# Encoder layer on eight cores: a smaller bias table expanded on the scalar engine, and normalising multiplies spread between attention items

## The chip, the cores and the metric

One Trainium2 chip, eight cores. The batch of 16 sequences is split by data: each core computes two whole sequences, one after the other, with its own copy of all weights, and exchanges nothing with the others. The time is the device time of the slowest core in microseconds. TensorE does the matrix products, VectorE (DVE) and ScalarE (ACT) the element-wise work and the copies out of PSUM, GpSimd (POOL) some element-wise work and the DMAs that change the type, and SyncE (SP) issues the other DMAs.

## The reference

Input x is 16 x 2048 x 1024, float32. One layer:

```
proj = x @ w_in                        # q, k, v of 24 heads, a Fourier branch, two gates
for g, (window, d) in ((128,1), (512,4), (2048,16)):     # 8 heads of 64 each
    query i sees keys i + m*d, |m| <= 64
    logits = q.k / 8 + bias[bucket(distance), head]
    out_g, lse_g = softmax(logits) @ v, log-sum-exp
attn = sum over g of softmax(lse)_g * out_g
four = real part of a 2-D DFT of the Fourier branch
mix  = (sig(gate_a) * (attn @ w_attn_out) + sig(gate_f) * (four @ w_fourier_out)) @ w_out
h    = layer_norm(alpha * x + mix)
out  = layer_norm(alpha * h + relu(h @ w_up + b_up)^2 @ w_down + b_down)
```

The merge of the three windows by their log-sum-exp equals one softmax over all keys of the three windows: numerators and denominators of the three can be added up and divided once at the end.

## The kernel before

A planner class records every operation with the buffers it reads and writes, and derives the semaphore waits from that; each engine then runs its list in the order in which the operations were recorded. Almost all operations go through small helpers, so most lines of the profile are those of a helper: 327 a matmul, 325 a matmul into a part of a bank, 330 a transpose, 316 and 317 a copy out of PSUM on ACT, 319 and 320 the same on DVE, 294 a DMA. SBUF is one pool with a stack of regions; a new region waits for the last users of whatever lay there before.

For each of the two sequences:

- x comes in 16 tiles of 128 tokens (SP queue, three buffers, 512 KB each). TensorE transposes a tile and, one tile later, multiplies it by the v weights of the first window (`v_chunk`, eight matmuls of 512 columns into one bank, copied out by ACT and DVE in turn). Two v weight blocks and the bias table are issued on the POOL queue ahead of that; the third v block needs the first one's buffer (lines 398 to 401).
- The bias table holds, for each of 24 heads, a block of 128 keys by 512 columns, with -30000 outside the band. A block of a head consists of two equal copies of 256 columns, for the widest window of four equal copies of 128. It is float32 in HBM and becomes bfloat16 in the DMA. After the first window's V, ACT takes the exponential of the whole table in place (line 432), then V of the other two windows follows, 16 chunks each.
- Attention runs over 12 pairs of heads: for each of four rounds `pp`, the windows g = 0, 1, 2. Before the items of a pair, TensorE runs the first two of its score products and then the q and k projection of the following pair (`proj`, 64 matmuls, evicted into `qk` by ACT and DVE in turn). An item is a bank of scores: TensorE computes it two items ahead, ACT takes the exponential (line 538), DVE multiplies it by the table (line 542), TensorE multiplies V by it (65 rows: 64 outputs and the denominator), and finished stretches of 512 positions are merged by DVE into `acc` (lines 570, 574, 579) one item later. A pair has 16 items for g = 0 and 1, 8 for g = 2.
- After the third window of a round, the denominators go through DRAM (`norm_dma`): stored, loaded as a 128 x 32 block, inverted on DVE, stored, and broadcast to 64 partitions in `rbc`. Eight multiplies of 64 x 512 (`norm_mul`, line 471) write `attnT`. They are recorded in the next pair, behind its projection and ahead of its items; for the fourth round, at the end of the attention stage.
- The q and k weights of each pair (`wqk`) come on the POOL queue with two buffers. In sequence 0 each of the first loads is followed by a cast of MLP weights from DRAM to DRAM (8 MB results for two of the three), in the same queue.
- Then the Fourier branch, the gated merge, the output projection, the layer norms and the MLP; they are not touched.

Of the kernel before, what the change touches and what calls it, by code (L numbers as in the profile page):

```python
# [7 lines left out]
BF16 = mybir.dt.bfloat16  # L8
AF = mybir.ActivationFunctionType
ALU = mybir.AluOpType  # L10
# [8 lines left out]
NEG = -30000.0  # L19
# [212 lines left out]
def build(debug=None, nseq=NSEQ):  # L232
    nc = bass.Bass("TRN2", target_bir_lowering=False)
    kb = KB(nc)
    mem = Mem(nc)

    def din(name, shape, dt=F32):
        return nc.dram_tensor(name, list(shape), dt, kind="ExternalInput").ap()
# [8 lines left out]
    wout_d = din("wout", [128, 8, D])  # L247
    wup_d = din("wup", [8, 128, 8, 512])
    wdn_d = din("wdn", [8, 128, 32, 128])
    tab_d = din("tab", [128, 24, 512])  # L250
    dft_d = din("dft", [4, 2, 128, 8, 512], BF16)
    c1024_d = din("c1024", [1, S], BF16)
    ccsc_d = din("ccsc", [128, 256], BF16)
# [30 lines left out]
    identf, identf_r, _ = palloc("identf", F32, [128])  # L284
    identb, identb_r, _ = palloc("identb", BF16, [128])
    onesf, onesf_r, _ = palloc("onesf", F32, [64])
    ccsc, ccsc_r, _ = palloc("ccsc", BF16, [256])
    pvec, pvec_r, _ = palloc("pvec", F32, [72])
    g2b, g2b_r, _ = palloc("g2b", F32, [D])
    b2b, b2b_r, _ = palloc("b2b", F32, [D])  # L290
    mhalf, mhalf_r, _ = palloc("mhalf", F32, [8])

    def dma(eng, out, in_, reads=(), writes=(), is_out=False):
        return kb.op(eng, lambda e: e.dma_start(out=out, in_=in_), reads, writes, dma=True, is_out=is_out)
# [78 lines left out]
    try:  # L373
        for s in range(nseq):
            mem.mark()
            mem.mark()
            xT, xT_r, _ = palloc("xT", BF16, [8, S], nres=16)
            attnT, attnT_r, _ = palloc("attnT", BF16, [4, S], nres=4)
            wf, wf_r, _ = palloc("wf", BF16, [8, 512], nres=1)

            xs, xs_r, _ = palloc("xs", F32, [3, D], nres=3, high=True)
            xs_ring = Ring(16, 3, lambda k, b: dma("sp", xs[:, b, :], x_d[s, k * 128:(k + 1) * 128, :],
                                                   writes=[xs_r[b]]))
# [9 lines left out]
            tab, tab_r, _ = palloc("tab", BF16, [24, 512])  # L393
            V, V_r, _ = palloc("V", BF16, [3, 16, 8, 65], nres=3)
# [3 lines left out]
            wv, wv_r, _ = palloc("wv", BF16, [2, 8, 512], nres=2)  # L398
            wv_ring = Ring(3, 2, lambda k, b: dma("pool", wv[:, b], wv_d[k], writes=[wv_r[b]]))
            wv_ring.need(0)  # L400
            dma("pool", tab, tab_d, writes=tab_r)

            def v_chunk(g, d, nkc, c):
                seg, kc = c // nkc, c % nkc
# [11 lines left out]
            for tt in range(16):  # L416
                xs_ring.need(tt)
                b = tt % 3
                for half in range(2):
                    bk, br = next_bank()  # L420
# [8 lines left out]
            v_chunk(0, 1, 16, 15)  # L429
            if debug is not None and debug[0] == "xT" and s == 0:  # L430
                finish_debug(xT, xT_r)
            kb.op("act", lambda e: e.activation(out=tab, in_=tab, func=AF.Exp), tab_r, tab_r)
            for g, (win, d) in enumerate(GROUPS):
                if g == 0:
                    continue
# [29 lines left out]
                dma("sp", rbc.rearrange("p e t -> p (e t)"), rden_s.to_broadcast([64, 2 * S]), reads=rden_sr, writes=rbc_r)  # L465

            def norm_mul(pp_):
                for e2 in range(2):
                    for tq in range(4):
                        cs = slice(tq * 512, (tq + 1) * 512)  # L470
                        kb.op("dve", (lambda cs, e2: lambda e: e.tensor_tensor(  # L471
                            out=attnT[64 * e2:64 * e2 + 64, pp_, cs], in0=acc[0:64, e2, cs], in1=rbc[:, e2, cs],
                            op=ALU.mult))(cs, e2), [acc_r[e2]] + rbc_r, [attnT_r[pp_]])

            pt_cnt = [0]
            pending_norm = None
# [2 lines left out]
            def proj(k):  # L479
                d = GROUPS[pairs[k][1]][1]  # L480
                wb = k % 2
                wqk_ring.need(k)
                for which in range(2):
                    for tq in range(4):
                        bk, br = next_bank()
                        for dc in range(8):
                            mm(bk[:, :], wqk[:, wb, which, dc, :], xT[:, dc, tq * 512:(tq + 1) * 512],
                               dc == 0, dc == 7, xT_r + [wqk_r[wb]], [br])
                        dst = qk[:, wb, which, :].rearrange("p (r l) -> p r l", r=d)[:, :, tq * 512 // d:(tq + 1) * 512 // d]
                        src = bk[:, :].rearrange("p (m r) -> p r m", r=d)  # L490
                        evac_copy(dst, src, [br], [qk_r[wb * 2 + which]], scale=(0.125 if which == 0 else None))
                        bfree(br)

            proj(0)
            for pair_i, (pp, g) in enumerate(pairs):
                if True:
# [96 lines left out]
                        it[0][1](it[1])  # L593
                    if pair_i + 1 < len(pairs):
                        proj(pair_i + 1)
                    if pending_norm is not None:
                        norm_mul(pending_norm)
                        pending_norm = None
                    pend = []
                    for ii, it in enumerate(items):  # L600
                        if ii + LA < len(items):
                            nx = items[ii + LA]
                            nx[0][1](nx[1])
                        pb = pt_cnt[0] % 3
                        pt_cnt[0] += 1
                        it[0][2](it[1], pb)
                        for mfn in pend:
                            mfn()
                        pend = []
                        it[0][3](it[1], pb, pend)  # L610
                    for mfn in pend:
                        mfn()
                if g == 2:
                    norm_dma()
                    pending_norm = pp
            norm_mul(pending_norm)
            mem.release()
            if debug is not None and debug[0] == "attnT" and s == 0:
                finish_debug(attnT, attnT_r)
# [330 lines left out]
def host_inputs(x, rel_bias, w_in, w_fourier_out, w_attn_out, w_out, ln1_g, ln1_b, w_up, b_up, w_down, b_down,  # L950
                ln2_g, ln2_b):
    f32 = np.float32
    w_in = np.asarray(w_in, f32)[0]
    Q, K_, V_, F_, GA, GF = 0, 1536, 3072, 4608, 5120, 6144

    def tile_w(w):
        return np.ascontiguousarray(w.reshape(8, 128, -1).transpose(1, 0, 2))

    wqk = np.stack([np.stack([tile_w(w_in[:, Q + 128 * p:Q + 128 * (p + 1)]),
                              tile_w(w_in[:, K_ + 128 * p:K_ + 128 * (p + 1)])]) for p in range(12)])  # L960
    wv = np.stack([tile_w(w_in[:, V_ + 512 * g:V_ + 512 * (g + 1)]) for g in range(3)])
    wf = tile_w(w_in[:, F_:F_ + 512])
    wg = np.stack([tile_w(w_in[:, GA + 128 * i:GA + 128 * (i + 1)]) for i in range(16)])
    wao = np.ascontiguousarray(np.asarray(w_attn_out, f32)[0].reshape(4, 128, D).transpose(1, 0, 2))
    wfo = np.ascontiguousarray(np.asarray(w_fourier_out, f32)[0].reshape(4, 128, D).transpose(1, 0, 2))
    wout = tile_w(np.asarray(w_out, f32)[0])
    wu = np.asarray(w_up, f32)[0]
    wup = np.stack([tile_w(wu[:, 512 * i:512 * (i + 1)]) for i in range(8)])
    wd = np.asarray(w_down, f32)[0]
    wdn = np.stack([np.ascontiguousarray(wd[:, 128 * dc:128 * (dc + 1)].reshape(32, 128, 128).transpose(1, 0, 2))  # L970
                    for dc in range(8)])
    rb = np.asarray(rel_bias, f32)
    i = np.arange(128)[:, None]
    j = np.arange(256)[None, :]
    rel = i - j + 64
    valid = np.abs(rel) <= 64
    tab = np.empty((128, 24, 512), f32)
    for g, (win, d) in enumerate(GROUPS):
        bk = t5_buckets(rel * d)
        for hh in range(8):  # L980
            h = 8 * g + hh
            t_ = np.where(valid, rb[bk, h], f32(NEG))
            if d == 16:
                tab[:, h, :] = np.tile(t_[:, 64:192], (1, 4))
            else:
                tab[:, h, :] = np.tile(t_, (1, 2))
    n = np.arange(S, dtype=np.int64)
    ang = 2.0 * np.pi * ((n[:, None] * n[None, :]) % S).astype(np.float64) / S
    cs = np.stack([np.cos(ang), np.sin(ang)]) / np.sqrt(S)
    c1024 = np.ascontiguousarray(cs[0, S // 2:S // 2 + 1, :]).astype(ml_dtypes.bfloat16)  # L990
    dft = cs[:, :S // 2].reshape(2, 8, 128, 4, 512).transpose(3, 0, 2, 1, 4)
    dft = np.ascontiguousarray(dft).astype(ml_dtypes.bfloat16)
    m = np.arange(128, dtype=np.int64)
    a2 = 2.0 * np.pi * ((m[:, None] * m[None, :]) % 128).astype(np.float64) / 128
    ccsc = (np.concatenate([np.cos(a2), -np.sin(a2)], axis=1) / np.sqrt(128.0)).astype(ml_dtypes.bfloat16)
    identf = np.eye(128, dtype=f32)
    identb = np.eye(128).astype(ml_dtypes.bfloat16)

    def pp(v):
        return np.asarray(v, f32).reshape(-1, 128).T  # L1000

    g1, b1 = np.asarray(ln1_g, f32)[0], np.asarray(ln1_b, f32)[0]
    pvec_parts = [pp(g1), pp(b1), None, None, pp(np.asarray(b_down, f32)[0]), pp(np.asarray(b_up, f32)[0])]
    shared = dict(wqk=wqk, wv=wv, wf=wf, wg=wg, wao=wao, wfo=wfo, wout=wout, wup=wup, wdn=wdn, tab=tab, dft=dft,
                  ccsc=ccsc, c1024=c1024, identf=identf, identb=identb,
                  g2b=np.ascontiguousarray(np.broadcast_to(np.asarray(ln2_g, f32)[0], (128, D))),
                  b2b=np.ascontiguousarray(np.broadcast_to(np.asarray(ln2_b, f32)[0], (128, D))))
    return shared, pvec_parts
# [26 lines left out]
```

How the kernel before makes its waits and increments, by code:

```python
        def run(e, eng):  # L119
            waited = {}
            for o in self.ops[e]:
                for d in o.deps:
                    if d.dma:
                        key, sem, val = ("d", d.sem), dsem[d.sem], d.val
                    else:
                        key, sem, val = ("e", d.eng), esem[d.eng], d.val
                    if waited.get(key, 0) >= val:
                        continue
                    waited[key] = val
                    eng.wait_ge(sem, val)
                ins = o.fn(eng)
                if o.dma:
                    ins.then_inc(dsem[o.sem], 16)
                elif o.signal:
                    ins.then_inc(esem[e], 1)
            if e == "sp":
                for sem, val in final_waits:
                    eng.wait_ge(sem, val)
```

## Time and profile before

| what | value |
|---|---|
| median of 10 runs | 2910.73 us (2907.38 to 3274.39) |
| profiled execution | 2907.47 us |
| its span on the slowest core (core 4) | 2905.9 us; the cores lie between 2883.3 and 2905.9 |
| TensorE matmul busy | 2465.3 us, 85% |
| DVE, ACT, POOL busy | 1138.6 (39%), 736.9 (25%), 153.8 (5%) |
| chain that ended last | PE 77%, DVE 8%, issue 5%, DMA 5%, ACT 2% |

The profile is one execution, seen from its slowest core. Busy time counts an engine's instructions; the chain follows the work that ended last back through its releasers. Matmuls are pipelined, so a busy TensorE is not one at its peak. An idle time before an instruction is given with what ended it, as far as semaphores show. The granted clock of TensorE is 1.00 at 2.4 GHz and 0.50 at 1.2 GHz; a stretch that shows something between has parts at both.

### The profile page before, as it was taken

How to read it: one execution, taken by the hardware profiler on the slowest of the kernel's cores; microseconds unless marked ns; L12 is line 12 of the kernel's file. 1: busy time of each engine (PE TensorE's matmuls, PEld its weight loads, DVE VectorE, ACT ScalarE, POOL GpSimd, SP SyncE). 2: the span in 40 equal slices, each digit the busy share in tenths (PEclk: the TensorE clock that was granted, in tenths of full speed). 3: DMA queues.
4: the chain of work that ended last, by engine and by line, in shares of the span. 5: the costliest groups of instructions: out<-in, count | busy, mean ns of one | idle time of the engine just before them, and what ended most of it. 6: DMA issues, size and time to landing. Idle time of an engine off the chain costs nothing.

```text
span 2905.9 us, 44223 instructions; the slowest of 8 cores (2883.3 to 2905.9 us)
## 1 busy us (share of the span) xinstructions
PE 2465.3 (85%) x11571; PEld 1168.3 (40%) x11784; DVE 1138.6 (39%) x2021; ACT 736.9 (25%) x1272; POOL 153.8 (5%) x189
## 2 busy tenths in 40 slices
PE   2884588887998999999946988888799989999995
PEld 1441233343443444444423533333344434444442
DVE  0222245542335345454321245545314454445442
ACT  0321132231222323232103132223212243223230
POOL 0000000000000001011010000000000000101011
PEclk9986777778999999999979977777899989999998
DMA  7699402124312244344355111100431133435342
GB/s 162 106 112 111 69 11 37 23 30 118 101 23 80 109 138 176 144 160 145 146 126 122 36 17 36 30 16 15 103 138 23 42 118 129 165 144 182 124 146 101
DMA packets 52442, 277.14 MB, mean 95 GB/s; under 512 B 7578, under 2 KB 7834, under 8 KB 30620
## 3 DMA queue, kind: packets, MB, share of 16 engines
q1 hardware_dynamic: 38676, 215.58, 21.5%
q0 software_dynamic: 13520, 58.72, 14.5%
q8 instruction: 101, 1.65, 0.2%
q14 instruction: 145, 1.19, 0.1%
HBM read 315.96 MB, written 35.91 MB: 121 GB/s over the span
## 4 chain that ended last, share of the span: by engine, by line
PE 77%; DVE 8%; issue 5%; DMA 5%; another core or an unknown queue 2%; ACT 2%; POOL 1%; DVEq 0%; SPq 0%; ACTq 0%; POOLq 0%
PE bank L327 67%; PE bank L325 7%; DMA pool<-x 2%; PE bank L330 2%; DVE pool L542 2%; DVE pool L471 1%; DVE pool L319 1%; ACT pool L316 1%; DVE pool L579 1%; ACT pool L538 1%; DMA pool<-den_s 1%; DMA pool<-rden_s 1%; DVE pool L764 1%; DMA pool<-wv 0%
## 5 line engine op out<-in xcount | busy, mean ns | idle before, releaser
L327 PE MATMUL bank<-pool 128*128 128x512 bf16 x9035 | 2059.6, 387 | 176.2 <-DMA pool<-wqk 69.7
L327 PEld LDWEIGHTS bank<-pool 128*128 128x128 bf16 x9248 | 930.3, 101 | 1276.3 <-issue 268.7
L325 PE MATMUL bank<-pool 64*128 64x256 bf16 (+7 forms) x1768 | 318.8, 322 | 137.1 <-DVE pool L542 112.8
L319 DVE CAST pool<-bank 128x512 bf16<-128x512 f32 x160 | 110.0, 693 | 495.0 <-PE bank L327 318.5
L325 PEld LDWEIGHTS bank<-pool 64*128 64x128 bf16 (+2 forms) x1768 | 144.4, 126 | 313.6 <-issue 306.1
L884 DVE TENSOR_SCALAR pool<-bank,pool 128x512 f32<-128x512 f32 x256 | 186.9, 748 | 172.9 <-PE bank L327 158.5
L316 ACT ACTIVATE pool<-bank 128x512 bf16<-128x512 f32 (+1 forms) x194 | 114.9, 597 | 530.0 <-PE bank L327 396.4
L888 ACT ACTIVATE pool<-pool 128x512 bf16<-128x512 f32 x256 | 160.2, 628 | 315.4 <-DVE pool L884 156.7
L538 ACT ACTIVATE pool<-bank 128x448 bf16<-128x448 f32 (+1 forms) x320 | 179.5, 570 | 200.6 <-PE bank L325 171.2
L330 PE MATMUL bank<-pool 128*128 128x128 f32 x768 | 107.2, 287 | 98.3 <-DMA pool<-x 79.3
L899 DVE SCALAR_TENSOR_TENSOR pool<-bank,pool 128x512 f32<-128x512 f32 x64 | 48.1, 751 | 328.1 <-PE bank L327 255.7
L330 PEld LDWEIGHTS bank<-pool 128*128 128x128 f32 x768 | 95.5, 149 | 118.4 <-issue 103.6
L715 ACT ACTIVATE pool<-bank 128x512 bf16<-128x512 f32 x128 | 76.2, 597 | 247.3 <-PE bank L327 244.4
L542 DVE TENSOR_TENSOR pool<-pool 128x448 bf16<-128x448 bf16 (+1 forms) x320 | 121.7, 403 | 33.8 <-ACT pool L538 32.8
L320 DVE TENSOR_SCALAR pool<-bank 128x512 bf16<-128x512 f32 x48 | 33.2, 691 | 238.0 <-PE bank L327 238.0
L723 DVE TENSOR_TENSOR pool<-bank,pool 128x512 f32<-128x512 f32 x64 | 44.3, 692 | 181.9 <-PE bank L327 181.9
L816 ACT ACTIVATE pool<-bank,pool 128x128 bf16<-128x128 f32 (+1 forms) x256 | 92.3, 469 | 51.3 <-PE bank L330 51.3
L317 ACT ACTIVATE pool<-bank 128x512 bf16<-128x512 f32 x48 | 28.7, 597 | 289.8 <-PE bank L327 289.8
L799 ACT ACTIVATE pool<-pool 128x1024 f32<-128x1024 f32 x32 | 39.7, 1240 | 223.1 <-DVE pool L775 223.1
L860 ACT ACTIVATE pool<-bank,pool 128x512 f32<-128x512 f32 x32 | 24.9, 778 | 255.4 <-DVE pool L856 198.6
L772 POOL TENSOR_TENSOR pool<-pool 128x1 f32<-128x1 f32 x64 | 35.1, 548 | 1028.6 <-DVE pool L769 1028.6
L822 DVE TENSOR_SCALAR pool<-bank,pool 128x128 bf16<-128x128 f32 (+1 forms) x256 | 84.4, 401 | 5.4 <-PE bank L330 2.7
(43 smaller groups left out, 683.4 us busy)
## 6 DMA issues: line engine op xcount, KB each, us to landing
pool<-wup_s SPq DMA_DIRECT2D x64, 1024.0 KB, 5.3
pool<-wdn_s SPq DMA_DIRECT2D x64, 1024.0 KB, 4.8
pool<-x SPq DMA_DIRECT2D x64, 512.0 KB, 4.0
pool<-dft SPq DMA_DIRECT2D x16, 1024.0 KB, 4.9
out<-pool SPq DMA_DIRECT2D x32, 512.0 KB, 2.9
pool<-wqk POOLq DMA_DIRECT2D x24, 512.0 KB, 6.5
wup_s<-wup POOLq DMA_DIRECT2D x1, 8192.0 KB, 117.6
wdn_s<-wdn POOLq DMA_DIRECT2D x1, 8192.0 KB, 132.0
```

Of the source, the lines that this page charges most:

```text
L316: return kb.op("act", lambda e: e.activation(out=out, in_=in_, func=AF.Copy), reads, writes)
L319: return kb.op("dve", lambda e: e.tensor_copy(out=out, in_=in_), reads, writes)
L325: return kb.op("pe", lambda e: e.matmul(out, lhsT, rhs, start=start, stop=stop, skip_group_check=True), reads, writes)
L327: return kb.op("pe", lambda e: e.matmul(out, lhsT, rhs, start=start, stop=stop), reads, writes)
L330: return kb.op("pe", lambda e: e.transpose(out, in_, identf), list(reads) + identf_r, writes)
L538: kb.op("act", lambda e: e.activation(out=PT[:, pb, c0:c1], in_=bk[:, c0:c1], func=AF.Exp), [br], [PT_r[pb]])
L542: kb.op("dve", lambda e: e.tensor_tensor(out=PT[:, pb, c0:c1], in0=PT[:, pb, c0:c1], in1=tcols, op=ALU.mult), [PT_r[pb]] + tab_r, [PT_r[pb]])
L715: kb.op("act", (lambda bk, gbuf, af: lambda e: e.activation(out=gts[:, gbuf, af, :], in_=bk[:, :], func=AF.Sigmoid))(bk, gbuf, af), [br], ...
L816: kb.op("act", (lambda bk, j, dc, dst, so, bo: lambda e: e.activation(out=dst, in_=bk[:, j * 128:(j + 1) * 128], func=AF.Identity, scale=p ...
L822: kb.op("dve", (lambda bk, j, dc, dst, so, bo: lambda e: e.tensor_scalar(out=dst, in0=bk[:, j * 128:(j + 1) * 128], scalar1=pvec[:, so + d ...
L884: kb.op("dve", (lambda bk, rb, fc: lambda e: e.tensor_scalar(out=rr[:, rb, :], in0=bk[:, :], scalar1=pvec[:, BUP + fc:BUP + fc + 1], scala ...
L888: kb.op("act", (lambda rb, fc: lambda e: e.activation(out=hidT[:, fc, :], in_=rr[:, rb, :], func=AF.Square))(rb, fc), [rr_r[rb]], [hidT_r[ ...
```

## The change

The table in HBM has one copy of 256 columns per head (24 x 256 in place of 24 x 512 per partition). It is loaded, still with the type changed in the DMA, into a new buffer `tabraw`, allocated behind `wv` and released with it; `qk` comes to lie on the same bytes later. The DMA is recorded after the first window's V, and on POOL's list it still stands between the second and the third v block. The single exponential becomes six: two write the two copies of the 16 heads of the first two windows (16 x 256 columns each), four write the four copies for the widest window from the middle 128 columns (8 x 128 columns each). All six write one resource of the planner.

`norm_mul` returns the eight multiplies as a list. In the pair that follows, two are taken from the list after the exponential and table multiply of each item and ahead of the pending merges, so that they are spread over the first four items. At the end of the attention stage they are run at once.

```
--- before.py
+++ after.py
@@ -247,7 +247,7 @@
     wout_d = din("wout", [128, 8, D])
     wup_d = din("wup", [8, 128, 8, 512])
     wdn_d = din("wdn", [8, 128, 32, 128])
-    tab_d = din("tab", [128, 24, 512])
+    tab_d = din("tab", [128, 24, 256])
     dft_d = din("dft", [4, 2, 128, 8, 512], BF16)
     c1024_d = din("c1024", [1, S], BF16)
     ccsc_d = din("ccsc", [128, 256], BF16)
@@ -398,7 +398,7 @@
             wv, wv_r, _ = palloc("wv", BF16, [2, 8, 512], nres=2)
             wv_ring = Ring(3, 2, lambda k, b: dma("pool", wv[:, b], wv_d[k], writes=[wv_r[b]]))
             wv_ring.need(0)
-            dma("pool", tab, tab_d, writes=tab_r)
+            tabraw, tabraw_r, _ = palloc("tabraw", BF16, [24, 256])
 
             def v_chunk(g, d, nkc, c):
                 seg, kc = c // nkc, c % nkc
@@ -429,7 +429,15 @@
             v_chunk(0, 1, 16, 15)
             if debug is not None and debug[0] == "xT" and s == 0:
                 finish_debug(xT, xT_r)
-            kb.op("act", lambda e: e.activation(out=tab, in_=tab, func=AF.Exp), tab_r, tab_r)
+            dma("pool", tabraw, tab_d, writes=tabraw_r)
+            for i in range(2):
+                kb.op("act", (lambda i: lambda e: e.activation(out=tab[:, 0:16, 256 * i:256 * i + 256],
+                                                                in_=tabraw[:, 0:16, :], func=AF.Exp))(i),
+                      tabraw_r, tab_r)
+            for i in range(4):
+                kb.op("act", (lambda i: lambda e: e.activation(out=tab[:, 16:24, 128 * i:128 * i + 128],
+                                                                in_=tabraw[:, 16:24, 64:192], func=AF.Exp))(i),
+                      tabraw_r, tab_r)
             for g, (win, d) in enumerate(GROUPS):
                 if g == 0:
                     continue
@@ -465,12 +473,14 @@
                 dma("sp", rbc.rearrange("p e t -> p (e t)"), rden_s.to_broadcast([64, 2 * S]), reads=rden_sr, writes=rbc_r)
 
             def norm_mul(pp_):
+                fns = []
                 for e2 in range(2):
                     for tq in range(4):
                         cs = slice(tq * 512, (tq + 1) * 512)
-                        kb.op("dve", (lambda cs, e2: lambda e: e.tensor_tensor(
+                        fns.append((lambda cs, e2: lambda: kb.op("dve", lambda e: e.tensor_tensor(
                             out=attnT[64 * e2:64 * e2 + 64, pp_, cs], in0=acc[0:64, e2, cs], in1=rbc[:, e2, cs],
-                            op=ALU.mult))(cs, e2), [acc_r[e2]] + rbc_r, [attnT_r[pp_]])
+                            op=ALU.mult), [acc_r[e2]] + rbc_r, [attnT_r[pp_]]))(cs, e2))
+                return fns
 
             pt_cnt = [0]
             pending_norm = None
@@ -593,8 +603,9 @@
                         it[0][1](it[1])
                     if pair_i + 1 < len(pairs):
                         proj(pair_i + 1)
+                    norm_fns = []
                     if pending_norm is not None:
-                        norm_mul(pending_norm)
+                        norm_fns = norm_mul(pending_norm)
                         pending_norm = None
                     pend = []
                     for ii, it in enumerate(items):
@@ -604,6 +615,9 @@
                         pb = pt_cnt[0] % 3
                         pt_cnt[0] += 1
                         it[0][2](it[1], pb)
+                        for _ in range(2):
+                            if norm_fns:
+                                norm_fns.pop(0)()
                         for mfn in pend:
                             mfn()
                         pend = []
@@ -613,7 +627,8 @@
                 if g == 2:
                     norm_dma()
                     pending_norm = pp
-            norm_mul(pending_norm)
+            for fn_ in norm_mul(pending_norm):
+                fn_()
             mem.release()
             if debug is not None and debug[0] == "attnT" and s == 0:
                 finish_debug(attnT, attnT_r)
@@ -974,16 +989,12 @@
     j = np.arange(256)[None, :]
     rel = i - j + 64
     valid = np.abs(rel) <= 64
-    tab = np.empty((128, 24, 512), f32)
+    tab = np.empty((128, 24, 256), f32)
     for g, (win, d) in enumerate(GROUPS):
         bk = t5_buckets(rel * d)
         for hh in range(8):
             h = 8 * g + hh
-            t_ = np.where(valid, rb[bk, h], f32(NEG))
-            if d == 16:
-                tab[:, h, :] = np.tile(t_[:, 64:192], (1, 4))
-            else:
-                tab[:, h, :] = np.tile(t_, (1, 2))
+            tab[:, h, :] = np.where(valid, rb[bk, h], f32(NEG))
     n = np.arange(S, dtype=np.int64)
     ang = 2.0 * np.pi * ((n[:, None] * n[None, :]) % S).astype(np.float64) / S
     cs = np.stack([np.cos(ang), np.sin(ang)]) / np.sqrt(S)
```

## Rows read from the trace of the kernel before

**Rows 1.** Page, costliest groups: names, shapes, count; busy us, mean ns; idle, releaser.

```profile
L327 PE MATMUL bank<-pool 128*128 128x512 bf16 x9035 | 2059.6, 387 | 176.2 <-DMA pool<-wqk 69.7
```

**Rows 2.** Waits of TensorE: waiter, releaser: us in total, times, longest us.

```profile
PE bank L325 <- DVE pool L542: 112.8, 118, 7.2
PE bank L330 <- DMA pool<-x: 79.3, 3, 44.3
```

**Rows 3.** Chain of waits, 0 to 420 us: start us, length us, what.

```profile
4.38 39.70 DMA pool<-x
...
119.65 10.74 PE bank L327 x49
...
270.22 45.06 another core or an unknown queue
```

**Rows 4.** Timeline of POOL, to 420 us: start, us, instruction [idle, releaser].

```profile
2.84 0.55 POOL L294 DMA_DIRECT2D pool<-tab  x1
110.86 0.53 POOL L294 DMA_DIRECT2D pool<-wv  x1 [107.48 <-PE bank L327]
```

**Rows 5.** DMA issues, to 60 us: count, KB each, us to landing.

```profile
pool<-tab POOLq DMA_DIRECT2D x1, 3072.0 KB, 38.3
```

**Rows 6.** Transfers of the tile wv, 0 to 60 us, issue to landing.

```profile
DMA to landing us min/median/max: 11.4/14.6/17.8
```

**Rows 7.** DMA queues, 20 to 28 us: packets, MB, time share.

```profile
q0 software_dynamic: 48, 1.18, 84.6%
q1 hardware_dynamic: 49, 0.20, 10.9%
```

**Rows 8.** DMA issues by line, 1490 to 1560 us.

```profile
pool<-tab POOLq DMA_DIRECT2D x1, 3072.0 KB, 23.1
```

**Rows 9.** Chain of waits, 1440 to 1640 us.

```profile
1517.38 22.35 DMA pool<-x
```

**Rows 10.** Timeline of TensorE, 1495 to 1545 us.

```profile
1539.87 1.94 PE L330 MATMUL bank<-pool 128*128 128x128 f32 x8 [11.51 <-DMA pool<-x]
```

**Rows 11.** Timeline of ACT, 104 to 135 us.

```profile
108.75 0.60 ACT L316 ACTIVATE pool<-bank 128x512 bf16<-128x512 f32 x1 [2.98 <-PE bank L327]
109.24 10.44 ACT L432 ACTIVATE pool<-pool 128x12288 bf16<-128x12288 bf16 x1
119.58 0.60 ACT L316 ACTIVATE pool<-bank 128x512 bf16<-128x512 f32 x1
```

**Rows 12.** Timeline of ACT, 1583 to 1615 us.

```profile
1586.52 0.60 ACT L316 ACTIVATE pool<-bank 128x512 bf16<-128x512 f32 x1 [2.98 <-PE bank L327]
...
1598.78 0.58 ACT L316 ACTIVATE pool<-bank 128x512 bf16<-128x512 f32 x1
```

**Rows 13.** Timeline of all engines, 336 to 384 us.

```profile
358.69 6.19 DVE L471 TENSOR_TENSOR pool<-pool 64x512 bf16<-64x512 f32 x8
364.92 1.06 DVE L542 TENSOR_TENSOR pool<-pool 128x448 bf16<-128x448 bf16 x3
...
365.46 15.15 PE L325 MATMUL bank<-pool 128*65 128x192 bf16 x68 [7.23 <-DVE pool L542]
...
370.23 0.69 DVE L570 COPY pool<-bank 65x512 f32<-65x512 f32 x1 [0.19 <-PE bank L325]
```

**Rows 14.** Timeline of all engines, 192 to 212.5 us.

```profile
196.30 2.81 PE L325 MATMUL bank<-pool 128*65 128x192 bf16 x19 [0.99 <-DVE pool L542]
...
199.74 0.69 DVE L570 COPY pool<-bank 65x512 f32<-65x512 f32 x1 [0.16 <-PE bank L325]
```

**Rows 15.** Transfers that read rden_s, 348 to 350 us, issue to landing.

```profile
DMA to landing us min/median/max: 9.0/9.0/9.0
```

**Rows 16.** Stretch: us, busy by engine, granted clock, DMA share, GB/s.

```profile
365.40:370.00 4.60, 4.54 (x21) 1.88 (x22) 2.42 (x6) 1.79 (x3) 0.00 (x0) 0.50 0.00 0
```

**Rows 17.** The same view, in the pair without a pending normalisation.

```profile
200.00:202.00 2.00, 2.00 (x11) 0.78 (x10) 1.30 (x4) 0.91 (x2) 0.00 (x0) 0.50 1.81 197
```

**Rows 18.** The same view, in a dense stretch of the MLP.

```profile
1200.00:1400.00 200.00, 196.98 (x939) 95.36 (x956) 98.94 (x185) 57.54 (x101) 26.87 (x28) 0.99 0.44 158
```

More of the change, by code:

```diff
@@ L249, in build @@
     wdn_d = din("wdn", [8, 128, 32, 128])
-    tab_d = din("tab", [128, 24, 512])
+    tab_d = din("tab", [128, 24, 256])
     dft_d = din("dft", [4, 2, 128, 8, 512], BF16)
@@ L400, in build @@
             wv_ring.need(0)
-            dma("pool", tab, tab_d, writes=tab_r)
+            tabraw, tabraw_r, _ = palloc("tabraw", BF16, [24, 256])
             def v_chunk(g, d, nkc, c):
@@ L431, in build @@
                 finish_debug(xT, xT_r)
-            kb.op("act", lambda e: e.activation(out=tab, in_=tab, func=AF.Exp), tab_r, tab_r)
+            dma("pool", tabraw, tab_d, writes=tabraw_r)
+            for i in range(2):
+                kb.op("act", (lambda i: lambda e: e.activation(out=tab[:, 0:16, 256 * i:256 * i + 256],
+                                                                in_=tabraw[:, 0:16, :], func=AF.Exp))(i),
+                      tabraw_r, tab_r)
+            for i in range(4):
+                kb.op("act", (lambda i: lambda e: e.activation(out=tab[:, 16:24, 128 * i:128 * i + 128],
+                                                                in_=tabraw[:, 16:24, 64:192], func=AF.Exp))(i),
+                      tabraw_r, tab_r)
             for g, (win, d) in enumerate(GROUPS):
@@ L467, in norm_mul @@
             def norm_mul(pp_):
+                fns = []
                 for e2 in range(2):
@@ L470, in norm_mul @@
                         cs = slice(tq * 512, (tq + 1) * 512)
-                        kb.op("dve", (lambda cs, e2: lambda e: e.tensor_tensor(
+                        fns.append((lambda cs, e2: lambda: kb.op("dve", lambda e: e.tensor_tensor(
                             out=attnT[64 * e2:64 * e2 + 64, pp_, cs], in0=acc[0:64, e2, cs], in1=rbc[:, e2, cs],
-                            op=ALU.mult))(cs, e2), [acc_r[e2]] + rbc_r, [attnT_r[pp_]])
+                            op=ALU.mult), [acc_r[e2]] + rbc_r, [attnT_r[pp_]]))(cs, e2))
+                return fns
             pt_cnt = [0]
@@ L595, in build @@
                         proj(pair_i + 1)
+                    norm_fns = []
                     if pending_norm is not None:
-                        norm_mul(pending_norm)
+                        norm_fns = norm_mul(pending_norm)
                         pending_norm = None
@@ L606, in build @@
                         it[0][2](it[1], pb)
+                        for _ in range(2):
+                            if norm_fns:
+                                norm_fns.pop(0)()
                         for mfn in pend:
@@ L615, in build @@
                     pending_norm = pp
-            norm_mul(pending_norm)
+            for fn_ in norm_mul(pending_norm):
+                fn_()
             mem.release()
@@ L976, in host_inputs @@
     valid = np.abs(rel) <= 64
-    tab = np.empty((128, 24, 512), f32)
+    tab = np.empty((128, 24, 256), f32)
     for g, (win, d) in enumerate(GROUPS):
@@ L981, in host_inputs @@
             h = 8 * g + hh
[L982 to L986, printed above, removed]
+            tab[:, h, :] = np.where(valid, rb[bk, h], f32(NEG))
     n = np.arange(S, dtype=np.int64)
```

## The prediction

> **What bounds the kernel now.** I read the page's list of costly groups first, to see what fills the time, then TensorE's waits, to see what it lacks, then the chain of waits and the timelines around the two places that the diff touches. The 9035 matmuls of line 327 hold 2059.6 of 2905.9 us [rows 1]; so whatever opens a gap in TensorE's stream is paid in full, and other engines matter only through such gaps. Of the gaps [rows 2], two belong to this change: 79.3 us in three waits for x tiles, and 112.8 us in 118 waits for line 542, the multiply by the bias table, with a longest of 7.2 us. A third kind, the wait for wqk behind the long cast jobs, the diff leaves alone, but it stands between the first gap and the end and must be followed.
>
> **The table's transfer, sequence 0.** TensorE starts when the first x tile lands, at 4.38 + 39.70 = 44.1 us [rows 3]. What holds a tile of 512 KB for 40 us? The table was issued at 2.84 [rows 4] and landed 38.3 us later, at 41.1 [rows 5]; the second wv load, issued just before it at about 2.3, took 17.8 us and landed near 20.1 [rows 6]. Between them the two queues moved 48 and 49 packets, but 1.18 MB against 0.20 [rows 7]: the engines take one packet from each in turn, a table packet (a row of 24 KB) is six times an x packet (4 KB), and so x and the two 512 KB constants ahead of it crawl until the table is through. With half the bytes the table still has 128 packets, one per partition, but of 12 KB. So as many packets of the other queue pass, and only the table's own time halves: 41.1 - 20.1 = 21.0 us, less the 10.9% in which the other queue moved [rows 7], 18.7, half of it 9.3. I take 9, since some of a landing does not shrink with the bytes.
>
> Does that reach the end? V of the first window follows at TensorE's pace, its end frees the wv buffer, and only then POOL issues the third wv load (110.86) with the casts behind it [rows 4]. That queue runs through to the fourth wqk load, for which TensorE stands 45.06 us from 270.22, until 315.3 [rows 3]. The queue begins 9 us earlier and ends 9 us earlier. The table's place on POOL's list is the same (after two wv loads, ahead of the third), so nothing is moved past anything there.
>
> The Trainium skill, DMA: Bandwidth & Descriptors, Anatomy of one DMA, fits 2.0 us plus bytes over 436 GB/s: by that the 1.57 MB saved in SBUF are worth 3.6 us a time, 7 for both sequences instead of 18. The trace moves 3.15 MB in some 18.7 us, 168 GB/s in SBUF bytes, and decides against it; the float source is twice as many bytes.
>
> **Sequence 1.** The same table takes 23.1 us [rows 8]; an x tile issued at 1517.38 lands 22.35 us later [rows 9], and TensorE stands idle for 11.51 us of that, until 1539.87 [rows 10]. Half of 23.1 less 10.9% is 10.3; I take 9 again. It stays below the 11.51 us of gap, so all of it counts, and after it no queue is late. Bounds for both together: 15 to 21 us, taken 18.
>
> **The expansion.** One activation of 128x12288 took 10.44 us from 109.24; the next eviction on ACT came at 119.58 [rows 11]. Six pieces hold as many elements. Each writes the whole table's resource, so each waits for the one before; five more starts at about 0.3 us (0.17 of fixed time, what the 0.60 us of an eviction of 512 columns holds beyond the slope of the long one, and a round through the own semaphore) make 1.5 us. What hides it: TensorE fills eight banks in rotation at 8 x 10.74/49 = 1.75 us each [rows 3], and the bank that ACT empties at 120.2 is needed again at 124.4 (the first chunk of the second window starts at 108.6, just before the eviction of the last chunk of the first at 108.75; that bank comes round again nine chunks on). That is 4.2 us of cover, in sequence 1 about 2.8 (1598.78 + 0.58 = 1599.4, against 1586.4 + 9 x 1.75 = 1602.2) [rows 12]. Cost nothing; a full microsecond more per piece would cost some 5 us in all. The raw table's bytes become part of qk's, so the first evictions into qk wait for the expansion, which ended 40 us before. The lower end: nothing is gained here.
>
> **The multiplies.** At the first pair of each later round, DVE runs eight multiplies of 0.68 us in one block of 6.19 us from 358.69, then three table multiplies in 1.06; TensorE idles 7.23 us until 365.46 [rows 13]. The same rows stand six times, three per sequence; the blocks at the ends of the sequences are drained at once as before. After the change DVE runs a table multiply, then two normalising ones, four times over. Start to start, from [rows 13]: table to normalising 0.33 ((1.06 - 0.41)/2), normalising to normalising 0.79, normalising to table 0.72: 1.84 a round. From 358.69, four rounds end at 366.05; the first merge into acc (0.69, line 570) follows, as it must, behind the last normalising multiply, and the fifth table multiply starts at 366.7 and ends at 367.1. The fifth item's P.V then ends at 367.7. Before, the merge that waits for that product started at 370.23, so it ended about 370.1. From there on TensorE is without gaps in both cases. Gain 2.4 to 2.5 us, not 7.2: DVE still owes 6.2 us before item five, and the items can lend it little idle time. Six times: 15 us.
>
> Bounds. If a table multiply does not overlap with its neighbours, a round is 2.1 us and the gain 1.5. The upper end is the pair without a pending normalisation: its same merge came at 199.74, 4.4 us after TensorE fell idle behind the projection (196.30 - 0.99) [rows 14], against 12.0 here (370.23 after 365.46 - 7.23): 7.6 us. The added wait: the first normalising multiply now sits behind one table multiply on DVE, and the later table multiplies behind it; it needs the broadcast reciprocals, issued at 348.66 and landed 9.0 us later, at 357.7 [rows 15], 1.3 us before it is due at 359.0. So it holds nothing up. TensorE's clock: after the stall it is granted 0.50, the 1.2 GHz level [rows 16]; with TensorE only trickling I expect the same fall.
>
> **Sum.** Against the profiled run (2907.5 us, span 2905.9): 18 + 15 = 33, giving 2874.5. That run lies 3.3 us below the median of 2910.7; on the median's scale 2878.
>
> **Rivals.**
> Starts only: DVE's total decides and the interleaved items end where they did; 2910.7 - 18 = 2893. For it: DVE has the same work to do. Against: today TensorE must catch up from 365.46, at the low clock, on work that could have been done meanwhile.
> Clock held: if TensorE, never idle for long, keeps the 2.4 GHz level, the pair costs what the one without normalisation does; 18 + 6 x 7.6 = 64, giving 2847. Against: after a gap of only 1 us the pair of [rows 14] falls to 0.50 too [rows 17].
> Transfer less halved: a large fixed part in the table's landing, starts worth 7 rather than 18; 22 in all, giving 2889.
> Slower: fuller cores are granted less clock. Place: the long dense stretches, now at 0.99 [rows 18]. Price: line 327's 2059.6 us [rows 1] at 0.97 instead of 1.00 cost 64 us, less 33 is 31 more, 2942; it decides from about 0.985. Against: dense stretches of 200 us ran at 0.99, and only 1% of idle time is taken out. The Trainium skill, TensorE: Matmul & The Clock Gate, Part 1, says that a die with three cores on dense matmuls is held at 13/16; that speaks for this one, and no dense stretch here shows it.
> Not as said: the x tile is held by the constants rather than the table and the multiplies stay tied to one another; no change, 2911. The packet counts speak against it.
>
> **How the numbers follow.** Forecast 0.65, starts only 0.14, clock held 0.07, transfer less halved 0.05, slower 0.05, no change 0.04. Faster by over 0.2% (5.8 us, about what a measurement of this kernel can tell from no change): 0.65 + 0.14 + 0.07 + 0.05 = 0.91; same 0.04; slower 0.05. The forecast's own range is 15 to 21 plus six times 1.5 to 3.5, so 24 to 42: 2869 to 2887. The range for 8 in 10 reaches up over the two weaker gains to 2897 and down half way to the held clock, 2860.
>
> **What would show it.** The first x tile lands at about 35 us, the table at 32; the wait for the fourth wqk load ends near 306; in sequence 1 the gap before tile five is near 2.5 us; TensorE never waits for ACT at the second window's V. At the six pairs, four rounds of one table and two normalising multiplies 1.84 us apart, TensorE's gaps about 1 us each, the next projection 2.5 us sooner. I am wrong if x still lands after 40 us, if the fifth P.V ends no sooner relative to the projection's end, or if the dense stretches show a clock under 0.98.

## The result, and the profile after

The changed kernel took 2872.94 us (median of 9 runs) where the kernel before took 2910.66 (32 runs): ratio 0.9861, 95% interval 0.985 to 0.9871, some 40 us. The forecast was 33 less, 2878. In some executions the cores of a die show a lower granted clock and take longer (the first profile of the changed kernel is one: 0.81 on core 3 from 2600 to 2800 us), and the ratios here leave those out, which is why the two medians differ by only 37.7. The rows below are from a second profile of the same kernel, a run of its own (2862.72 us, ratio 0.9862, 0.9843 to 0.9881), core 1, its slowest.

The page, and under it TensorE's waits (total us, times, longest us), answer to [rows 1, 2]:

```profile
span 2860.2 us, 44215 instructions; the slowest of 8 cores (2844.4 to 2860.2 us)
...
L327 PE MATMUL bank<-pool 128*128 128x512 bf16 x9248 | 2078.7, 387 | 154.0 <-DMA pool<-wqk 65.7
```

```profile
PE bank L325 <- DVE pool L552: 102.8, 145, 1.8
PE bank L327 <- DMA pool<-wqk: 65.7, 2, 43.3
PE bank L330 <- DMA pool<-x: 58.8, 4, 34.0
```

Line 552 is the old 542, the multiply by the table. Its longest wait fell from 7.2 to 1.8 us, while the sum only fell from 112.8 to 102.8: more and shorter waits. x cost 20.5 us less. A matmul of line 327 still lasts 387 ns, and the dense stretches of the MLP are granted 0.99 and 1.00 (the column behind the engines' busy times), as before [rows 18]:

```profile
1200.00:1400.00 200.00, 195.85 (x943) 93.72 (x942) 99.31 (x185) 59.60 (x104) 26.88 (x28) 0.99 0.41 148
2600.00:2800.00 200.00, 195.84 (x947) 93.50 (x946) 91.86 (x170) 56.39 (x99) 23.26 (x24) 1.00 0.42 151
```

Sequence 0: the chain, and the issues of the first 60 us (KB of one, median us to landing), which answer to [rows 3, 5, 6]:

```profile
4.59 29.16 DMA pool<-x
...
258.08 43.20 another core or an unknown queue
301.41 15.97 PE bank L327 x64
```

```profile
pool<-wv POOLq DMA_DIRECT2D x2, 1024.0 KB, 14.2
pool<-tab POOLq DMA_DIRECT2D x1, 1536.0 KB, 27.8
```

The first x tile lands at 33.75 instead of 44.1, the table 27.8 us after issue instead of 38.3, and the wait for the fourth wqk load ends at 301.4 instead of 315.3. The two queues from 20 to 28 us (packets, MB, share), as in [rows 7]:

```profile
q0 software_dynamic: 96, 1.16, 82.8%
q1 hardware_dynamic: 98, 0.39, 17.9%
```

Still one packet for one: in the same 8 us the table's queue moved 1.16 MB where it had moved 1.18, now in 96 packets of 12 KB, and the other queue got 98 turns instead of 49.

POOL's DMA issues (first the third wv load of sequence 0, then the loads of sequence 1) and, under them, TensorE in sequence 1 at the sixth tile, which the prediction calls tile five, counting from 0 (start, length, what, idle before and its releaser; [rows 10] before).

```profile
100.94 0.53 POOL L294 DMA_DIRECT2D pool<-wv  x1 [97.56 <-PE bank L327]
...
1471.86 1.17 POOL L294 DMA_DIRECT2D pool<-wv  x2 [3.56 <-PE bank L330]
1473.01 0.55 POOL L294 DMA_DIRECT2D pool<-tab  x1
```

```profile
1498.66 1.89 PE L327 MATMUL bank<-pool 128*128 128x512 bf16 x8 [1.20 <-ACT pool L316]
1501.58 1.06 PE L330 MATMUL bank<-pool 128*128 128x128 f32 x8 [1.03 <-DMA pool<-x]
```

The gap is 1.03 us instead of 11.51 (over the eight cores 0.83 to 2.42 instead of 9.99 to 13.11). From the first V matmul to the table's exponential it is 64.6 us (1484.58 to 1549.16), before 75.4 (1512.99 to 1588.43).

ACT at the expansion, against [rows 11]:

```profile
99.31 7.32 ACT L434 ACTIVATE pool<-pool 128x4096 bf16<-128x4096 bf16 x2
106.72 4.50 ACT L438 ACTIVATE pool<-pool 128x1024 bf16<-128x1024 bf16 x4
111.13 0.58 ACT L316 ACTIVATE pool<-bank 128x512 bf16<-128x512 f32 x1
```

Six pieces in 11.8 us, 1.4 over the single piece of 10.44. From 96 to 180 us TensorE has no wait for ACT, and none from 1545 to 1600 us in sequence 1.

The first of the six pairs, all engines in order of time, against [rows 13] (L480 is the normalising multiply, L580 the merge):

```profile
344.66 0.39 PE L325 MATMUL bank<-pool 64*128 64x256 bf16 x2
...
345.51 0.38 DVE L552 TENSOR_TENSOR pool<-pool 128x448 bf16<-128x448 bf16 x1
345.81 1.47 DVE L480 TENSOR_TENSOR pool<-pool 64x512 bf16<-64x512 f32 x2
...
347.20 0.41 DVE L552 TENSOR_TENSOR pool<-pool 128x512 bf16<-128x512 bf16 x1
347.53 1.46 DVE L480 TENSOR_TENSOR pool<-pool 64x512 bf16<-64x512 f32 x2
...
347.75 0.70 PE L325 MATMUL bank<-pool 128*65 128x256 bf16 x5 [1.05 <-DVE pool L552]
...
352.83 0.69 DVE L580 COPY pool<-bank 65x512 f32<-65x512 f32 x1
353.44 0.75 DVE L552 TENSOR_TENSOR pool<-pool 128x512 bf16<-128x512 bf16 x2
...
354.41 0.69 DVE L580 COPY pool<-bank 65x512 f32<-65x512 f32 x1 [0.22 <-PE bank L325]
```

One table multiply, two normalising ones, a round every 1.69 to 1.96 us, and TensorE waits about 1 us in each. TensorE's granted clock over the pair (the column behind the engines' busy times; the last two are DMA):

```profile
344.70:349.00 4.30, 1.72 (x12) 0.67 (x11) 3.89 (x8) 1.59 (x3) 0.70 (x1) 1.00 0.50 74
349.00:352.00 3.00, 1.46 (x9) 0.68 (x10) 2.80 (x5) 0.80 (x2) 0.00 (x0) 0.64 0.37 69
352.00:366.00 14.00, 12.34 (x57) 4.88 (x57) 9.91 (x22) 5.81 (x10) 0.00 (x0) 0.50 0.00 1
```

It falls to 0.50, the 1.2 GHz level, as it did before [rows 16]: the held clock did not come.

### The profile page after: what moved, and what is told of

Read it like the earlier page. It is cut to its first block, busy times and chain, and to the rows that moved or that the text cites. A ratio compares the mean times of both kernels' runs of the same rounds, so it can differ in the third digit from the quotient of the medians.

```text
span 2911.7 us, 44215 instructions; the slowest of 8 cores (2869.7 to 2911.7 us)
## 1 busy us (share of the span) xinstructions
PE 2521.8 (87%) x11784; PEld 1178.9 (40%) x11784; DVE 1137.8 (39%) x2021; ACT 741.0 (25%) x1282; POOL 153.8 (5%) x189
## 4 chain that ended last, share of the span: by engine, by line
PE 78%; DVE 7%; issue 5%; DMA 4%; another core or an unknown queue 2%; ACT 2%; POOL 1%; DVEq 0%; SPq 0%; ACTq 0%; POOLq 0%
PE bank L327 70%; PE bank L325 6%; PE bank L330 2%; DVE pool L552 2%; DMA pool<-x 2%; DVE pool L319 1%; DVE pool L480 1%; DVE pool L589 1%; ACT pool L316 1%; ACT pool L548 1%; DMA pool<-den_s 1%; DMA pool<-rden_s 1%; DMA den_s<-pool 0%; DVE pool L779 0%
## 5 line engine op out<-in xcount | busy, mean ns | idle before, releaser
L327 PE MATMUL bank<-pool 128*128 128x512 bf16 x9248 | 2126.4, 393 | 155.0 <-DMA pool<-wqk 67.6
L327 PEld LDWEIGHTS bank<-pool 128*128 128x128 bf16 x9248 | 940.4, 102 | 1307.1 <-issue 421.5
L325 PE MATMUL bank<-pool 64*128 64x256 bf16 (+7 forms) x1768 | 311.8, 317 | 126.3 <-DVE pool L552 102.9
```

The costliest lines, as they stand in the source:

```text
L325: return kb.op("pe", lambda e: e.matmul(out, lhsT, rhs, start=start, stop=stop, skip_group_check=True), reads, writes)
L327: return kb.op("pe", lambda e: e.matmul(out, lhsT, rhs, start=start, stop=stop), reads, writes)
```

## The experiments

Diffs are against the changed kernel. Gains are the ratio's distance from 1 times about 2908 us, the median of before beside these runs.

**The changed kernel once more** (full_again), beside its halves. No edit.

> The whole change once more, beside its two halves on the same chip. Sum theory (table and multiplies each keep their own gain): 38 to 42 us below before, as first measured. For the profile: the first x tile lands at 35 us; in sequence 1 TensorE waits less than 1 us for the x tile that cost it 11.5 us, because POOL issues the raw table right behind the two wv loads; the 15.9 us that POOL spent ahead of the old table's DMA are gone.

Ratio 0.9862 (0.9843 to 0.9881), 40 us: what the halves below must add up to.

**The table alone** (table_only): small table and expansion, all eight multiplies in one block.

```
-                        norm_fns = norm_mul(pending_norm)
+                        for fn_ in norm_mul(pending_norm):
+                            fn_()
```

> The small table with its expansion, the eight multiplies in one block as before. Sum theory: 9 us at the start of sequence 0 and 11 at the start of sequence 1, some 20 us below before (ratio 0.993). Rival, the multiplies bring nothing and the table all of it: 40 us below (0.986). Rival, the table's fixed part dominates: 7 us below (0.9975).

2886.1 us, ratio 0.9935 (0.992 to 0.9949): 18.9 us; the block is back (6.19 us on DVE, TensorE idle for 7.23). The table's term was 18.

**The multiplies alone** (multiplies_only): the old table and its single exponential, the multiplies spread.

```
-    tab_d = din("tab", [128, 24, 256])
+    tab_d = din("tab", [128, 24, 512])
-            tabraw, tabraw_r, _ = palloc("tabraw", BF16, [24, 256])
+            dma("pool", tab, tab_d, writes=tab_r)
...
+            kb.op("act", lambda e: e.activation(out=tab, in_=tab, func=AF.Exp), tab_r, tab_r)
```

> The spread multiplies with the old table. Sum theory: 2.4 us at each of six pairs, 15 us below before (0.995); if the measured 40 us is all to be shared by the two halves, up to 20 us. Rival, DVE's total decides and spreading moves nothing: within 2 us of before. Rival, the pair falls back to the cost of one without pending multiplies: 45 us below (0.985).

2883.31 us, ratio 0.993 (0.9914 to 0.9945): 20.4 us, where the term was 15. The halves sum to 39 of 40: they don't share a gain. "Starts only" (18 in all) falls, and "transfer less halved" (7 for the starts) falls with the run before.

**One multiply per item** (one_per_item): over eight items instead of four.

```
-                        for _ in range(2):
+                        for _ in range(1):
```

> The whole change, but one multiply after each of the first eight items in place of two after each of the first four. Theory (DVE's start-to-start times set the rounds): a round is 0.33 + 0.72 = 1.05 us, under the 1.1 us that TensorE needs for an item at its lower clock, so DVE no longer holds TensorE up; the pair ends some 2.5 us sooner than with two per item, 15 us in all, ratio to before 0.981. Rival, only DVE's total of 6.2 us counts: as the whole change, 0.986. Rival, the clock then holds longer as well: 0.976 or less.

2847.8 us, ratio 0.9799 (0.9783 to 0.9816): 58.5 us, 18 more than the changed kernel. DVE and TensorE (core 2) at the first pair:

```profile
345.63 0.38 DVE L552 TENSOR_TENSOR pool<-pool 128x448 bf16<-128x448 bf16 x1
345.93 0.68 DVE L480 TENSOR_TENSOR pool<-pool 64x512 bf16<-64x512 f32 x1
346.53 0.41 DVE L552 TENSOR_TENSOR pool<-pool 128x512 bf16<-128x512 bf16 x1
```

```profile
347.08 0.70 PE L325 MATMUL bank<-pool 128*65 128x256 bf16 x5 [0.26 <-DVE pool L552]
348.02 0.71 PE L325 MATMUL bank<-pool 128*65 128x64 bf16 x5 [0.24 <-DVE pool L552]
```

For the first four items a round is 0.9 us, an item's P.V 0.70, TensorE's gaps 0.25 instead of 1.05. From the fifth item on a merge joins the multiplies on DVE, and TensorE waits again, 1.01, 0.68 and 0.65 us; the clock falls as with two per item (0.65 from 349 to 352 us, then 0.50):

```profile
350.68 2.26 PE L325 MATMUL bank<-pool 128*65 128x64 bf16 x10 [1.01 <-DVE pool L552]
```

From the pair's first score products to the next pair's it is 34.9 us; with two per item 37.6 (344.66 to 382.24), with the block 40.6 (357.85 to 398.49). So what bounds the interleaved items is DVE's list between two table multiplies, as the prediction had it, and the later items have room for more of it, though not for all: "DVE no longer holds TensorE up" holds for the first four items only.

**The table issued late again** (late_issue). The trace after showed something that the prediction had not: before, POOL let 16 us pass in sequence 1 between the wv loads and the table. POOL, the kernel before, core 4:

```profile
1499.28 1.17 POOL L294 DMA_DIRECT2D pool<-wv  x2 [3.56 <-PE bank L330]
1516.37 0.53 POOL L294 DMA_DIRECT2D pool<-tab  x1 [15.91 <-PE bank L327]
```

After, the table follows wv at once. The old buffer overlaps buffers that the MLP of sequence 0 had used, and in the kernel's lists its load carries 257 semaphore waits; `tabraw` lies elsewhere, and its load carries 2. To see whether the waits make the 16 us, and whether the 16 us make the gain, the small table's load gets the old buffer's dependencies as well:

```
-            dma("pool", tabraw, tab_d, writes=tabraw_r)
+            dma("pool", tabraw, tab_d, writes=tabraw_r + tab_r)
```

> The whole change, but the raw table's DMA also declared a writer of the table's buffer, so that in sequence 1 POOL again passes 257 waits, all long satisfied, ahead of it. Theory (the 15.91 us that POOL stood ahead of the old table's DMA in sequence 1, on all cores alike, are those waits at some 62 ns each): POOL is idle about 15.9 us between the wv loads and the raw table, the table lands later, and TensorE waits 2 to 4 us for the x tile instead of 1. Rival (the 15.91 us were a full descriptor ring or a fetch held up by traffic): POOL issues the table right away, as in the whole change.

This run has no ratio; its trace is read, on core 4:

```profile
1484.49 0.53 POOL L294 DMA_DIRECT2D pool<-tab  x1 [16.03 <-PE bank L327]
```

```profile
1478.56 3.16 PE L327 MATMUL bank<-pool 128*128 128x512 bf16 x8 [10.91 <-DMA pool<-wv]
...
1499.54 1.06 PE L330 MATMUL bank<-pool 128*128 128x128 f32 x8 [1.93 <-DMA pool<-x]
```

The 16 us are back on all eight cores, 16.03 on each, whatever TensorE is doing there, so the waits make them. But they cost nothing: the sixth tile comes in time, the seventh 1.93 us late (1.03 and, on core 4, 2.42 us at the sixth in the changed kernel), and from the first V matmul (1478.56) to the exponential (1543.23) it is 64.7 us, as in the changed kernel (64.6, on core 4 64.8). I had taken the earlier issue for a part of the gain in sequence 1; that falls. With the half size the gap closes wherever the load is issued.

**x first** (x_first). In sequence 0 TensorE still stands 34 us for x. Four constants are moved behind the first x loads, and the table waits for the ninth transposed x tile:

```
-    dma("sp", g2b, g2b_d, writes=g2b_r)
-    dma("sp", b2b, b2b_d, writes=b2b_r)
...
+            if s == 0:
+                rest_consts()
...
-            dma("pool", tabraw, tab_d, writes=tabraw_r)
+            dma("pool", tabraw, tab_d, reads=[xT_r[8]], writes=tabraw_r)
```

> The whole change, with the first x tiles ahead of the constants that are needed late, and the raw table's load held back until the ninth x tile has been transposed. Theory (queues take turns packet by packet, so what counts is how many packets stand ahead of x and how large the other queue's are): the first x tile lands at 14 to 16 us instead of 34, the next two within 6 us; sequence 0 gains some 18 us, sequence 1 one; ratio 0.979 to 0.981. Rival, the software queue goes first altogether: x lands when the second wv load is through, 20 us, gain 14 us. Rival, the held-back table now comes late for its exponential or starves later x tiles: no gain over the whole change, 0.986.

2858.54 us, ratio 0.9838 (0.9823 to 0.9853): 7 us less than the changed kernel instead of 18; the intervals overlap a little. TensorE (core 3) shows where the rest went, and under it the chain's piece for the last of the three tiles (from issue to landing):

```profile
15.52 1.94 PE L333 MATMUL bank<-pool 128*128 128x128 f32 x8 [15.52 <-DMA pool<-x]
23.52 1.94 PE L333 MATMUL bank<-pool 128*128 128x128 f32 x8 [6.05 <-DMA pool<-x]
...
73.15 1.16 PE L333 MATMUL bank<-pool 128*128 128x128 f32 x8 [3.64 <-DMA pool<-x]
```

```profile
58.61 14.41 DMA pool<-x
```

The first x tile comes at 15.5, 18.2 us sooner than in the changed kernel. But TensorE now waits 6.05 us for the second, and the table, issued at 56.16, holds a later tile for 14.41 us on its way, of which TensorE waits 3.64. That leaves 8.5 us; the third wv load goes out 7.8 us sooner (mean of eight cores), which fits the 7 measured. A part of the transfer's cost was moved, not hidden.

**One wait per semaphore** (fewer_waits). Where an instruction waits for several values of one semaphore, only the highest is kept.

```
+                best = {}
...
+                    if key not in best or best[key][1] < val:
+                        best[key] = (sem, val)
+                for key, (sem, val) in best.items():
```

> The whole change, but every operation waits once per semaphore, for the highest value, instead of passing a rising series of values. Theory (a satisfied wait costs its engine some 50 to 60 ns): POOL's 3.56 us ahead of the wv loads in sequence 1 fall to under 1, TensorE starts that sequence's V 3 us sooner, and other engines gain a little; 3 to 10 us below the whole change, ratio 0.983 to 0.985. Rival, satisfied waits cost nothing that counts: 0.986.

Ratio 0.985 (0.9835 to 0.9864), about 3.5 us below the changed kernel's, and the intervals overlap: not told apart from nothing. POOL (core 6) stands no more ahead of wv, but TensorE still waits:

```profile
1470.33 1.26 POOL L886 TENSOR_TENSOR pool<-pool 128x512 f32<-128x512 f32 x1
1471.54 1.17 POOL L298 DMA_DIRECT2D pool<-wv  x2
```

```profile
1486.38 3.19 PE L331 MATMUL bank<-pool 128*128 128x512 bf16 x7 [10.23 <-DMA pool<-x]
```

3.56 us gone at POOL; TensorE's gap in that place goes from 12.72 to 10.23, with x named in the place of wv. In the mean of eight cores the first V matmul starts 43.0 us behind the MLP's last long run of matmuls, where it was 43.4.

**These three together** (all_together): one per item, one wait per semaphore, x first. The diffs are those above.

> One multiply per item, x ahead of the late constants with the table held back, and one wait per semaphore. If the gains are independent: 40 + 18 + 18 + 5 = 81 us below before, ratio 0.972. Rival, they share the same slack (the wait for the fourth wqk load swallows what sequence 0 gains ahead of it): 0.978.

2832.7 us, ratio 0.9745 (0.9729 to 0.9761). That is 74 us, where 40, 18, 7 and 3.5 make 69: within the intervals the gains add up, and the wait for the fourth wqk load swallows none of them. x_first's new waits are in it too.

**The table behind nearly all x tiles** (table_after_x). As x_first, but the load waits for the 14th tile and the exponentials stand behind the second window's V:

```
+            dma("pool", tabraw, tab_d, reads=[xT_r[13]], writes=tabraw_r)
...
+                if g == 1:
+                    for i in range(2):
+                        kb.op("act", (lambda i: lambda e: e.activation(out=tab[:, 0:16, 256 * i:256 * i + 256],
```

> As x_first, but the raw table waits for the fourteenth x tile instead of the ninth, and its exponentials follow the second window's V. Theory (in x_first the held-back table met x tiles that were still to come and made one of them 14.4 us late, packet for packet): the third v load is issued near 82 us instead of 94, x tiles wait for nothing after the third; with 4 to 5 us lost to the steady wait before, ratio 0.979 to 0.981. Rival, the 14.4 us were the constants or the casts: no gain over x_first, 0.984.

2849.72 us, ratio 0.9807 (0.9791 to 0.9822), 16 us below the changed kernel's. POOL, and TensorE's waits for x up to 120 us (core 5):

```profile
76.85 0.53 POOL L294 DMA_DIRECT2D pool<-tab  x1 [74.01 <-DVE pool L322]
88.52 0.53 POOL L294 DMA_DIRECT2D pool<-wv  x1 [11.14 <-PE bank L330]
```

```profile
PE bank L333 <- DMA pool<-x: 21.2, 2, 15.0
```

No later x tile is starved any more: 15.0 us for the first and 6.2 for the second, which is thus not the table's doing; what holds the second no run separates. (The 14.4 us of the expectation are the load's, of which TensorE waited 3.64.) The third wv load, with which the long queue begins, goes out at 88.52 instead of 100.94, and most of these 12 us reach the end. This is the chain of the prediction's first step, pushed further, and it holds.

**All of it** (best_of_all): one per item, one wait per semaphore, the table behind x, and in sequence 1 the first loads of x and wv moved ahead of the second layer norm's tail.

```
+    for eng, lo, hi, mark in hoists:
...
+        at = next(i for i, o in enumerate(rest) if o.idx >= mark)
+        kb.ops[eng] = rest[:at] + moved + rest[at:]
```

> All of it: one multiply per item, one wait per semaphore, x first and the table after x, and in sequence 1 the first three x loads and two wv loads issued ahead of the last layer norm's stores and of POOL's part in it. If TensorE's 23 us for x and some 10 us for wv at the seam of the sequences shrink to what the layer norm's own tail leaves: 15 to 20 us below all_together, with 7 us at the start of sequence 0 some 25 us; ratio 0.965 to 0.967. Rival, the tail of the layer norm (the statistics that share bytes with the transposed x) holds the evictions back as long as x did: 0.972.

2822.26 us, ratio 0.9711 (0.9696 to 0.9725): 84 us below before, the fastest version run. The move of the loads brought less than the 15 to 20 us expected: by the sum of the single edits (0.9862 less 0.0063, 0.0012 and 0.0055 is 0.9732) it is worth 0.0021, 6 us, and against all_together (0.9745, less the 0.0031 between table_after_x and x_first) 1 us, neither of them clear of the intervals. By the traces it is 8 us: the first V matmul starts 35.3 us behind the MLP's last long run of matmuls, where it was 43.2 in table_after_x (means of eight cores). TensorE's waits from 1395 to 1500 us, core 5:

```profile
PE bank L334 <- DVE pool L326: 26.0, 5, 21.0
```

The waits for x and wv have become one of 21.0 us for an eviction by DVE, which stands in DVE's list behind the layer norm's tail.

## Why the prediction was right, step by step

- Table, sequence 0: 9 us forecast, about 10 found at the first x tile (44.1 to 33.75) and 10.5 in the table's landing; the packet turns are as argued. The row "table at 32, x at 35" came to 31 and 33.75. The fourth wqk wait ends at 301.4 instead of "near 306"; 14 us sooner than before is more than the start gave, since the queue itself was 4 us shorter on this core (200.3 us from the third wv load against 204.4). That is not the table's: in the mean of eight cores the queue took 202.7 us before, 199.3 in multiplies_only with the same old table and 200.0 here.
- Table, sequence 1: 9 us forecast, 10.8 found (75.4 to 64.6), nearly all of the 11.51 us gap. Both starts: 18 forecast, 18.9 measured alone (15 to 23 by its interval). The estimate from the fit in the Trainium skill, DMA: Bandwidth & Descriptors, Anatomy of one DMA, was 7 us for both; the measurement decides against it.
- Expansion: nothing, as forecast; 1.4 us longer on ACT (1.5 forecast), no wait of TensorE behind it. The first eviction into `qk` came 62 us behind it (111.2 to 173.1), not 40, which changes nothing.
- Multiplies: the mechanism was right, the size a quarter too small (15 of 20.4); this is the mis-sized term. Rounds of 1.84 us were forecast (1.69 to 1.96 found), the fifth table multiply 8.0 us behind the first (353.44 - 345.51 = 7.9), and the merge that waits for the fifth P.V 2.4 to 2.5 us sooner: it starts 9.75 us behind the pair's first score product (354.41 - 344.66) where it was 12.38, so 2.6. What failed is "from there on TensorE is without gaps in both cases": the idle time before the last items went from 0.53 to 0.25 us, and from pair to pair the gain is 3.06 us (40.64 to 37.58). Six times that is 18.4. The two pairs behind each, which have no normalising multiplies, gain too: 61.45 us in multiplies_only where they took 61.75 before (means over eight cores), 1.8 in six; why is not shown. That makes 20.2, and the run alone measured 20.4 (16 to 25). The 3.5 us a pair at the upper end of the forecast's range had no row behind it.
- Rivals: starts only, transfer less halved, held clock and no change are ruled out by the two halves and the clock rows. Slower cores too: line 327 stays at 387 ns and the dense stretches at 0.99 and 1.00. The Trainium skill, TensorE: Matmul & The Clock Gate, Part 1, states a limit of 13/16 once three cores of a die run dense matmuls; in these stretches, with eight cores at work, it does not show.

What I got wrong afterwards weighs more than the forecast's 7 us: in sequence 1 I took POOL's early issue for a cause (late_issue says no), and of x_first I expected 18 us where it gave 7, since I had counted the first tile's 18 us and followed neither the second tile (6.05 us) nor the table's transfer into the next wait (3.64 us).

## What to carry to other kernels

When a small load waits behind a large one on another queue, count packets before bytes: here the turns went one for one, so halving the large one's packet gave the other twice the packets in the same 8 us (49 to 98), and its load landed after 29.2 us instead of 39.7. When off-path work is spread between items, spread it until one item's share is below that item's time on the engine that bounds: one multiply per item gave about twice the gain of two (a pair of 34.9 us instead of 37.6, from 40.6). And a transfer moved off one stall must be followed to where it lands, as must a wait that goes: in three of these runs the stall came back under another name.

## What the runs showed beside

A semaphore wait that is already satisfied is not free on POOL: 257 of them took 15.91 us and 72 took 3.56, some 62 and 50 ns each, alike on every core; late_issue's load has 259 and took 16.03. On most cores the profile names TensorE as the releaser there, and TensorE had long been done with what these loads wait for; the stretch returned when only the list of waits was restored, and the 3.56 us went when one wait per semaphore was kept. It cost nothing that shows in these places; what it costs on an engine that bounds, no run here shows.
